# Head norm of four attention mixers: rotation before the head scale, head scale moved from GpSimd to VectorE

## The reference, cut to what matters

```
def rms_norm(x, g):
    return x * rsqrt(mean(x * x, axis=-1) + 1e-6) * g

# A, B: whole head rotated, latent tokens only
q, k = rms_norm(q, q_norm), rms_norm(k, k_norm)
q, k = apply_rope(q, ang), apply_rope(k, ang)
# C: k = concat(k_nope, kr of the token, the same for all heads); only the last 32 columns rotated
# D: norm only, no rotation
# apply_rope: (x0, x1) -> (x0 cos - x1 sin, x0 sin + x1 cos) on neighbouring pairs
new_k = normed, unrotated keys of the context tokens (A, B, D)
```

## Time and profile before

| what | value |
|---|---|
| median of 3 runs (lowest, highest) | 3345.8 us (3342.89, 3345.81) |
| profiled execution, its own time | 3347.13 us |
| its span, first to last instruction | 3345.2 us |
| mean granted PE clock, share of full | 0.947 |
| PE / PEld / DVE / ACT / POOL busy | 2967.0 / 2870.6 / 2190.8 / 1271.6 / 218.5 us |
| mixer A, its 16 batches | about 414 to 518 us of the span |
| mixer B | about 1185 to 1290 us |
| mixer C | about 1982 to 2158 us |
| mixer D | about 2821 to 3017 us |

### The profile page before, as it was taken

How to read it: one execution, slowest core, us unless ns; L and a number is a source line. 1 busy time by engine, 2 the same in 40 slices (tenths; PEclk the granted TensorE clock), 3 DMA queues, 4 the chain that set the end, 5 groups by cost and what they waited for, 6 DMA issues and landing times.

```text
span 3345.2 us, 43719 instructions
## 1 busy us (share of the span) xinstructions
PE 2967.0 (89%) x17407; PEld 2870.6 (86%) x17407; DVE 2190.8 (65%) x3134; ACT 1271.6 (38%) x1841; POOL 218.5 (7%) x195
## 2 busy tenths in 40 slices
PE   2998688999999788999999767799999996778999
PEld 2998668999899777999999766689999996668999
DVE  8778686666777766666677745466767776455543
ACT  2332354442333254442332245444323323443542
POOL 0000120000000020000000024200000002220000
PEclk9999899999999898999999888899999998889999
DMA  5555312554455311455355411035535553212442
GB/s 204 201 198 211 137 41 77 187 204 177 147 193 214 147 60 64 177 192 196 143 189 209 171 35 35 32 144 188 206 127 205 198 204 134 82 58 97 154 144 88
DMA packets 86771, 491.19 MB, mean 147 GB/s; under 512 B 10624, under 2 KB 10944, under 8 KB 51200
## 3 DMA queue, kind: packets, MB, share of 16 engines
q1 hardware_dynamic: 82816, 481.46, 38.6%
q0 software_dynamic: 3840, 8.24, 0.9%
HBM read 486.37 MB, written 3.29 MB: 146 GB/s over the span
## 4 chain that ended last, share of the span: by engine, by line
issue 46%; PE 29%; DVE 15%; ACT 7%; POOL 3%; ACTq 0%; DMA 0%; DVEq 0%; SPq 0%; POOLq 0%
PE ps L709 7%; DVE ps L1225 5%; PE ps L741 5%; ACT w_hi L976 5%; PE ps L713 4%; PE ps L689 4%; PE ps L721 3%; PE ps L694 2%; DVE w_lo L1203 1%; ACT L976 1%; DVE tmp L1266 1%; POOL C_cat L582 1%; DVE tmp L1298 1%; PE ps L789 1%; DVE h_lo L1256 1%
## 5 line engine op out<-in xcount | busy, mean ns | idle before, releaser
L1203 DVE TENSOR_TENSOR w_lo<-w_raw,w_hi 128x2048 fp32r<-128x2048 f32 (+3 forms) x282 | 712.4, 2526 | 529.5 <-ACT w_hi L976 529.5
L689 PE MATMUL ps<-h_hi,w_hi 128*128 128x384 f32 x2688 | 901.7, 335 | 3.7 <-ACT w_hi L976 3.5
L689 PE MATMUL ps<-h_lo,w_hi 128*128 128x384 f32 x2688 | 898.3, 334 | 0.0
L1225 DVE CUSTOM_DVE_ANT_0 ps<-F_slab,cond,mod_b 128x1024 f32<-128x1024 f32 x544 | 684.6, 1308 | 0.0
L976 ACT ACTIVATE w_hi<-w_raw 128x2048 fp32r<-128x2048 f32 (+3 forms) x282 | 587.2, 2082 | 16.9 <-DMA w_raw<-in_a_w 5.9
L689 PEld LDWEIGHTS ps<-h_hi,w_hi 128*128 128x128 f32 x2688 | 504.5, 188 | 10.6 <-ACT w_hi L976 4.8
L689 PEld LDWEIGHTS ps<-h_lo,w_hi 128*128 128x128 f32 x2688 | 504.6, 188 | 0.0
L709 PE MATMUL ps<-F_act_hi,w_hi 128*128 128x384 f32 x1408 | 476.6, 338 | 21.2 <-ACT w_hi L976 13.9
L694 PE MATMUL ps<-h_hi,w_lo 128*128 128x384 f32 x2688 | 493.1, 334 | 0.0
L709 PE MATMUL ps<-F_act_lo,w_hi 128*128 128x384 f32 x1408 | 474.9, 337 | 0.0
L694 PEld LDWEIGHTS ps<-h_hi,w_lo 128*128 128x128 f32 x2688 | 468.3, 188 | 0.0
(11 more groups left out here) (294 smaller groups left out, 3502.0 us busy)
## 6 DMA issues: line engine op xcount, KB each, us to landing
w_raw<-in_ffn_gu SPq DMA_DIRECT2D x176, 1024.0 KB, 4.8
F_slab<-in_mod_w SPq DMA_DIRECT2D x272, 512.0 KB, 5.6
w_raw<-in_ffn_dn SPq DMA_DIRECT2D x64, 1408.0 KB, 6.4
w_raw<-in_d_w SPq DMA_DIRECT2D x8, 1536.0 KB, 6.8
boot<-in_mod_w SPq DMA_DIRECT2D x7, 1024.0 KB, 7.7
w_raw<-in_a_w SPq DMA_DIRECT2D x4, 1536.0 KB, 6.7
w_raw<-in_b_w SPq DMA_DIRECT2D x4, 1536.0 KB, 6.7
w_raw<-in_c_w SPq DMA_DIRECT2D x8, 544.0 KB, 3.6
```

The costliest lines, as they stand in the source:

```text
L689: pe.matmul(ps[:, 2 * par + u, 0:N_TOK], w[0][:, k, u, :], h[:, k, :], start=(k == 0 and h is h_hi), stop=False)
L1203: dve.tensor_tensor(w_lo[par][:, 0:w], w_raw[par][:, 0:w], w_hi[par][:, 0:w], ALU.subtract).then_inc(w_split_lo.sem, 1)
L1225: dve.tensor_tensor_reduce(out=junk, in0=w, in1=cond[:, c, :], scale=scale, scalar=mod_b[:, n:n + 1], op0=ALU.mult, op1=ALU.add, accum_out ...
```

## The change

1. POOL keeps only the power (`hrs`). Its multiplications of the heads (L575, L582, L584) and its copies of the rotary key into each group (L621) are gone.
2. DVE's `head_norm` becomes three functions. `head_sums` makes `hms`. `rotate_heads` rotates the unscaled heads (with the weights folded into cos and sin; nothing in D), so it doesn't wait for POOL. `scale_heads` waits for `hrs` and multiplies once by the head scale (in C three operations, in A and B one and the copy of the key, in D one and a small one, `kout`, for the key output).
3. In C and D the norm weights of unrotated columns are applied by ACT in the copies of the transposes, as a scale that is one number for each partition (`gT`, a new input of 128 x 2).
4. In C the rotary key is the same in every group: it is weighted, squared, summed and rotated once (`rotary_key`), and queries and keys lie in tiles of their own.
5. Order on DVE. In D, `scale_heads(g+1)` moves to the even batch, ahead of `split_lo`, and the bias of the next group to the odd batch. In C, `rotate_heads` stands in the even batch and `scale_heads` in the odd one, behind `maximum`. In A and B the rotation stands in the second batch and the scale in the third. `split_lo` now stands ahead of `o_lo`.
6. Order on ACT. `split_hi` of chunk g+3 moves ahead of a `raw`: in C and D ahead of both tiles of the even batch, in A and B ahead of the one tile of the second batch.

```diff
@@ GpSimd
-                    scale_heads(s, g)
-                    if kind == "C" and g + 2 < GROUPS[kind]:
-                        pool.wait_ge(qkt_made.sem, qkt_made.after((s, g), 3))
-                        rotary_key(g + 2)
...
@@ ScalarE
+                    if kind in "AB":
+                        act.activation(dst, src, ACT.Copy).then_inc(qkt_ready.sem, 1)
+                    else:
+                        j = 0 if what == "q" else 1
+                        act.activation(dst, src, ACT.Copy, scale=v["gT"][0:w, j:j + 1]).then_inc(qkt_ready.sem, 1)
...
                     if len(later) == 2:
                         probabilities(s, b)
+                        for c in chunks_split(kind, b):
+                            split_chunk(nd + c)
                         raw(s, *later[0])
...
                     if b < BATCHES and len(later) < 2:
                         probabilities(s, b)
+                    if len(later) < 2:
+                        for c in chunks_split(kind, b):
+                            split_chunk(nd + c)
                     if later:
                         raw(s, *later[-1])
-                    for c in chunks_split(kind, b):
-                        split_chunk(nd + c)
...
@@ VectorE
+            def scale_heads(s, g):
...
+                dve.wait_ge(hrs_ready.sem, hrs_ready.after((s, g)))
+                if g >= 1:
+                    p = g * per_pair(kind) - 1
+                    dve.wait_ge(qkt_made.sem, qkt_made.after((s, p), len(qkt_types(kind, p)) - 1))
+                if kind == "C":
...
+                    dve.tensor_tensor(qn[:, 0:TT, 0:2, :], v["qraw"][g % 2][:], by(0, 6, C_QK), ALU.mult)
+                    dve.tensor_tensor(qn[:, :, 2:4, 0:C_NOPE], v["kraw"][g % 2][:], by(6, 8, C_NOPE), ALU.mult)
+                    dve.tensor_tensor(qn[:, :, 2:4, C_NOPE:C_QK],
+                                      v["krr"][:].unsqueeze(2).to_broadcast([P, 4, 2, C_ROPE]), by(6, 8, C_ROPE),
+                                      ALU.mult).then_inc(qn_ready.sem, 1)
+                    return
+                if g >= 1:
+                    dve.wait_ge(kv_out, kv_sent[s, g - 1])
...
                 for b in range(BATCHES + 3):
+                    g, i = divmod(b, 2 * per)
+                    norm_next = g + 1 < n_g
                     if b < BATCHES:
-                        g, i = divmod(b, 2 * per)
+                        maximum(s, b)
+                    if norm_next and per == 1:
                         if i == 0:
-                            ahead = head_norm(s, g + 1) if g + 1 < n_g else iter(())
-                            if kind == "D":
-                                head_bias(s, g)
-                        maximum(s, b)
-                    if per == 1:
-                        next(ahead, None)
+                            head_sums(s, g + 1)
+                        elif kind == "C":
+                            scale_heads(s, g + 1)
                     if 1 <= b < BATCHES + 1:
                         inverse(s, b - 1)
+                    if norm_next:
+                        if per == 2 and i == 0:
+                            head_sums(s, g + 1)
+                        if i == per - 1:
+                            rotate_heads(s, g + 1)
+                        if (kind == "D" and i == 0) or (per == 2 and i == 2):
+                            scale_heads(s, g + 1)
+                        if kind == "D" and i == 1:
+                            head_bias(s, g + 1)
+                    for c in chunks_split(kind, b):
+                        split_chunk(nd + c)
                     if b >= 4 and b % 2 == 0:
                         o_lo(s, b // 2 - 2)
-                    if per == 2:
-                        next(ahead, None)
-                    for c in chunks_split(kind, b):
-                        split_chunk(nd + c)
```

More of the change, by code:

```diff
@@ L436, in build @@
                     if kind == "D":
+                        v["gT"] = part("gT", [P, 2])
+                        v["kout"] = part("kout", [P, 2 * HD])
                         v["bias"] = [part(f"bias{i}", [P, 2, 6, GRID_W]) for i in range(2)]
@@ L647, in _ @@
                         pool.wait_ge(qn_ready.sem, qn_ready.after((s, g)))
-                        pool.dma_start(out[f"new_{kind.lower()}_k"][:, g * kw:(g + 1) * kw],
-                                       v["qn"][:, 0, HPG[kind] * HD:HPG[kind] * HD + kw]).then_inc(kv_out, 16)
+                        key = v["kout"][:] if kind == "D" else v["qn"][:, 0, HPG[kind] * HD:HPG[kind] * HD + kw]
+                        pool.dma_start(out[f"new_{kind.lower()}_k"][:, g * kw:(g + 1) * kw], key).then_inc(kv_out, 16)
                         pool.dma_start(out[f"new_{kind.lower()}_v"][:, g * kw:(g + 1) * kw],
@@ L1035, in squares_of @@
                     if g >= 1:
-                        act.wait_ge(qn_ready.sem, qn_ready.after((s, g - 1)))
+                        done = hms_ready if kind == "D" else qn_ready
+                        act.wait_ge(done.sem, done.after((s, g - 1)))
                     nn = (HPG[kind] + KVPG[kind]) * HD
@@ L1321, in mixer_constants @@
                 dve.wait_ge(mixer_in, n_loads[kind])
+                if kind == "C":
+                    tail = v["g"][:, 0, C_NOPE:C_QK]
+                    chain.link(dve.tensor_tensor(v["cg"][:], v["cos"][:], tail.unsqueeze(1).to_broadcast([P, 2, C_ROPE]),
+                                                 ALU.mult))
+                    g2 = tail.rearrange("p (e two) -> p e two", two=2)
+                    sg, sin = (v[n].rearrange("p t (e two) -> p t e two", two=2) for n in ("sg", "sin"))
+                    for e in range(2):
+                        other = g2[:, :, 1 - e].unsqueeze(1).to_broadcast([P, 2, C_ROPE // 2])
+                        chain.link(dve.tensor_tensor(sg[:, :, :, e], sin[:, :, :, e], other, ALU.mult))
                 if kind in "AB":
@@ L1389, in head_norm @@
-                lat = v["nrm"][:, 1:3, :]
+                nh = HPG[kind] + KVPG[kind]
+                src = v["raw"][g % 4][:, :, 0:nh * HD] if kind == "D" else v["nrm"][:]
+                r = v["hrs"][:, 0:TT * nh].rearrange("p (t h) -> p t h", h=nh).unsqueeze(3)
+                chain.link(dve.tensor_tensor(qn[:, :, 0:nh * HD].rearrange("p t (h d) -> p t h d", h=nh),
+                                             src.rearrange("p t (h d) -> p t h d", h=nh),
+                                             r.to_broadcast([P, TT, nh, HD]), ALU.mult))
@@ new lines, in scale_heads, with rotary_key @@
+                if kind == "D":
+                    cols = slice(HPG[kind] * HD, nh * HD)
+                    dve.tensor_tensor(v["kout"][:], qn[:, 0, cols], v["g"][:, cols], ALU.mult).then_inc(qn_ready.sem, 1)
+                else:
+                    dve.tensor_copy(qn[:, :, nh * HD:(nh + 1) * HD], qn[:, :, (nh - 1) * HD:nh * HD]
+                                    ).then_inc(qn_ready.sem, 1)
+            def rotary_key():
+                v = tiles["C"]
+                kr, krr, r = v["kr"], v["krr"], v["rope"].rearrange("p t h d -> p (t h) d")
+                chain.link(dve.tensor_tensor(krr[:], kr[:], kr[:], ALU.mult))
+                chain.link(dve.tensor_reduce(v["krsq"][:], krr[:], AX.X, ALU.add))
+                gain = v["g"][:, 1, C_NOPE:C_QK].unsqueeze(1).to_broadcast([P, 4, C_ROPE])
+                chain.link(dve.tensor_tensor(krr[:], kr[:], gain, ALU.mult))
@@ L1398, in head_norm @@
-                dve.tensor_copy(qn[:, :, nh * HD:(nh + 1) * HD], qn[:, :, (nh - 1) * HD:nh * HD]
-                                ).then_inc(qn_ready.sem, 1)
+                    chain.link(dve.tensor_tensor(r[:, 0:2].rearrange(pair, two=2)[:, :, :, e],
+                                                 krr[:, 1:TT].rearrange(pair, two=2)[:, :, :, 1 - e],
+                                                 v["sin"].rearrange(pair, two=2)[:, :, :, e], ALU.mult))
+                chain.link(dve.tensor_tensor(krr[:, 1:TT], krr[:, 1:TT], v["cos"][:], ALU.mult))
@@ L1401, in head_bias @@
+                chain.link(dve.tensor_tensor(krr[:, 1:TT], krr[:, 1:TT], r[:, 0:2], ALU.add))
             def head_bias(s, g):
@@ L1500, in compress @@
                                   v["ckT_hi"][:, :, N_TOK:N_TOK + N_PAST], ALU.subtract).then_inc(c_t_ready, 1)
+                rotary_key()
             chain.link(dve.memset(ssq[:], 0.0))
```

181 lines of the change are left out of this document (80 added, 101 removed).

## The result

The changed kernel takes 3256.6 us (median of 4 runs, 3252.9 to 3261.8) beside 3345.1 us before: ratio 0.974, 95% interval 0.972 to 0.976, so 88.5 us less. The profiled execution took 3261.8 us, with a span of 3260.0. The forecast was 3280, with 3262 to 3308 as its range: the sign is right, the gain is a third larger than forecast and lies outside the range.

What follows compares the result with a forecast made beforehand. It took chains of waits, with no engine full, to bound C and D. D 35.5, C 28.9, copies -2.4, A and B 4 make 66.0 us off 3347.1: 3281.1 profiled, 3280 as median, range 3262 to 3308.

Steps and rivals of the forecast that it cites:

- The clock: TensorE's low clock after D's waits: 1.75 us a group could come back; 0.9 was counted, nothing in the other mixers.
- the new 1.8 us hole: In D, TensorE's new wait for the projection tile, since the moved `split_hi` delays the first `raw`: 1.8 us a group.
- Rival 1: Clock comes back altogether with the waits gone: 5.4 us more in D, 10.4 in C, 3264 us; chance 0.13.
- D's idle time: D's 6.65 us wait goes, 1.8 comes back: net 4.9 us a middle group; D 35.5 us with clock.
- D's last group: `o_lo` now stands behind the scale and `split_lo`; `values` end 7.9 us after `hms` instead of 9.0: 1.1 us gained.
- C: With POOL out of the chain to `turn_qk`, its waits shrink: 1.95 us gained in the examined group, 28.9 in all.
- the first wait: Wait before C's first `turn_qk`: the scale ends at 1976.1 instead of 1982.53, 6.4 us gained.
- Copies: ACT's scaled transpose copies in C and D cost 0.095 us more each: 2.4 us lost, bounds nothing and 4.6.
- A and B: DVE gets 1.15 us more work a group, but `maximum` stands behind less: 4 us gained for both, bounds +9 and -12.
- Rivals 2 to 4: Rival 2, Rival 4, and between them DVE's in-order list becoming the bound: 3366 us, chance 0.04 together with Rival 4.
- Rival 2: The `raw` delayed by the moved `split_hi` holds TensorE longer in C and D, gain only 34 us: 3312 us; chance 0.18.
- Rival 4: TensorE held at the low clock through D, 12 us a group longer: about 3390 us; 0.04 together with the DVE-bound rival.

Runs made afterwards that it cites:

- run 1: Kernel before, with only ScalarE's new order (`split_hi` of chunk g+3 ahead of the raw copies): 3299.1 us, ratio 0.986.
- run 4: Kernel before, with unread transposes ahead of TensorE's wait for the heads (20 in D, 10 in C), filling 2.4 us in D: 3343.0 us, ratio 0.999.
- Experiment 5: Kernel before, with 44 unread transposes in D and 26 in C, filling nearly all of TensorE's wait for the heads: 3327.8 us, ratio 0.994.
- run 7: Changed kernel, with C's rotation moved behind `maximum`, directly ahead of the scale: 3263.4 us, ratio 0.976.
- run 6: Changed kernel, with the old head norm in A and B alone: 3266.8 us, ratio 0.977.
- experiments 1 to 3: run 1, run 2 and a third: the changed kernel with ScalarE's old order and `o_lo` ahead of `split_lo`, 3260.6 us, ratio 0.974.
- run 2: Changed kernel, with `split_hi` back in its old place on ScalarE, behind the raw copies: 3285.8 us, ratio 0.982.
- experiment 11: Changed kernel, with `split_hi` between the two raw copies in C and D, not ahead of both: 3236.4 us, ratio 0.967.
- run 8: Changed kernel, with all of `scale_heads` on GpSimd in all four mixers, behind VectorE's early rotation: 3259.5 us, ratio 0.974.

## Why the prediction missed, by its own steps

- **The clock: the step that failed.** The prediction worked out 1.75 us a group in D, took "the middle, 0.9", because "the new 1.8 us hole may lower the clock as well", and counted nothing in C, A and B: 5.4 us in the sum. The runs showed 25.3 us over the four mixers (9.5 in D, 6.6 in C, 9.2 in A and B). In the steady groups the new hole did not lower the clock: 1.51 us of wait in D at a clock of 1.00, and in run 1 two holes (1.07 and 1.51 us), also at 1.00, while the 2.93 us left in run 4 still did. Experiment 5 shows that the clock is a cause and no companion: with every instruction waiting for what it waited for before, filling the wait gives 17.9 us.
- **The fear behind the halving was not empty.** Holes of 3.15 and 2.32 us in D's first two groups and 2.64 us in C's sixth are followed by matmuls at the low level again, and run 7 has the same waits once at 1.00 and once at 0.91. A longer hole need not do it either: in run 1 D's second group starts behind 2.90 us and runs at 1.00. What was wrong was to charge it to each steady group, and to leave three mixers out. The Trainium skill, "TensorE: Matmul & The Clock Gate", § HAM oscillation — how this bites in real kernels, has a wait that recurs with every tile bring the low clock back each time. The trace agrees for the 6.65 us of the steady groups of D before (clock 0.87 in each), and shows 1.00 in each when 1.51 us take their place.
- **Rival 1 had the mechanism and nearly the price** (3264 us). It had 10.8 us of clock in D and 10.4 in C, where 9.5 and 6.6 were measured (11.0 in C by the profile of run 6). Its 0.13 was too low. It left A and B out, where another 9.2 us of busy time went.
- **D's idle time: right in size, incomplete in its cause.** Forecast 30.1 less 0.8 for the copies, measured 30.2. The new wait for `raw` was 1.51 us against 1.8. The text gave the wait's end to the scale standing ahead of the queue; experiments 1 to 3 show that this alone does not cure it (run 2: groups of up to 27.2 us), that ScalarE's order alone nearly does, and that the position of `o_lo`, which the prediction followed only in the last group, decides whether the old order on ScalarE would have been enough. D's last group gained 2.8 us against 1.1, though `o_lo` behind `split_lo` does cost, as forecast (4.5 us of wait).
- **C: right.** Idle 28.0 against 27.3; the first wait 6.7 against 6.4. The steady group lost 5.27 us: 3.0 of idle (5.35 to 2.35), where waits of 4.5 less 1.1 less 0.5 gave 2.9, and 2.27 of clock, which was not counted.
- **Copies: about right.** 2.0 us by the groups of the profile against 2.4; the runs can't tell it from nothing.
- **A and B: right in sign, too small.** 5.6 us of idle and 9.2 of clock against 4, beyond the bound of 12. Why the first group needs both edits was not taken further.
- **Rivals 2 to 4 did not come.** VectorE is busy 13.40 of 20.69 us in D. Rival 2's delay exists (experiment 11: it costs some 20 us), but inside a net gain. Rival 4's 12 us a group do not follow from its own figures: 38 less 27.5 is 10.5.
- Groups came out at 20.7 and 17.0 us, where 21.7 and 19.5 were named, and GpSimd lost 91 us, where 120 were named.

## What to carry to other kernels

When a wait of TensorE recurs in every group and the rows behind it show matmuls at half speed, price that slowed work as part of the wait, in full, for every stage in which it recurs. Then go through the holes that stay or are new, group by group: here 1.5 us in the steady groups of D left the clock at 1.00 and 6.65 lowered it in each, while holes of 1.8 to 3 us went either way from group to group. If a long in-order operation feeds a queue, list all that stands behind it, not just the operand whose wait the profile names: curing the named one (the heads) showed the next (`o_lo`) with the same price. And a copy that frees a PSUM bank for TensorE should go ahead of a long operation on its engine when that operation's consumer has slack.

## What was not expected of the hardware

Filling TensorE's waits with useless transposes made the whole kernel 0.6% faster (interval of the ratio 0.992 to 0.996), although most groups of C and D then hold 3 to 5 us more work. Filling less than half of D's waits gave nothing that the runs can tell.

GpSimd and VectorE held each other up in run 8, and in each case looked at the one that started first kept its usual time. In A GpSimd's multiplication kept its 1.80 us and VectorE's split, started beside it, took 5.00 instead of 3.36. GpSimd's copy of 192 columns, started during that split, took 3.35 us and ended 0.2 us behind it; alone it took 0.34. In D's first group the split kept 3.36 us and the multiplication of 768 columns, started during it, took 3.74 instead of 1.47. So a small multiplication can take longer than a large one: the key output of D, 128 columns, took 3.46 us beside a split, and 1.06 in the first group, where no split ran. Spans on GpSimd are rough in this profiler, so of these figures the split's, which is VectorE's, carries the most weight. That the first to start holds the other is worked out from these few cases, and no run tests it.

```profile
411.27 0.34 POOL L603 COPY A_qn<-A_qn 128x192 f32<-128x192 f32 x1
...
2870.07 3.55 DVE L1221 TENSOR_TENSOR w_lo<-w_raw,w_hi 128x3072 fp32r<-128x3072 f32 x1 [2.49 <-ACT w_hi L988]
...
2870.49 3.46 POOL L601 TENSOR_TENSOR D_kout<-D_qn,D_g 128x128 f32<-128x128 f32 x1
```
